# A transformer trunk layer on one core: the gate-and-up projections with the weight tiles stationary and the activations moving

## The chip, the cores and the metric

One core of a Trainium2 chip runs the whole layer in one launch. The metric is the device time of one execution in microseconds (us): the median of several runs of the same kernel. A profile is one execution, recorded instruction by instruction; its span runs from the first to the last instruction on the core.

## What is computed

The layer takes `x` (256 tokens of width 2048) and 256 memory tokens, all in float32. The change touches the two feed-forward blocks, one at the start and one at the end of the layer (`D_FF` is 5632):

```python
def rmsnorm(x, w):
    xf = x.astype(jnp.float32)
    y = xf * lax.rsqrt(jnp.mean(xf * xf, axis=-1, keepdims=True) + EPS)
    return (y * w.astype(jnp.float32)).astype(x.dtype)

def swiglu(x, w_gu, w_down):
    g, u = jnp.split(x @ w_gu, 2, axis=-1)
    return (jax.nn.silu(g) * u) @ w_down

h = h + 0.5 * rmsnorm(swiglu(rmsnorm(h, n_ffn1_pre), w_ffn1_gu, w_ffn1_down), n_ffn1_post)
# ... mixer: gated linear attention, gated delta rule, cross-attention, output projection ...
h = h + 0.5 * rmsnorm(swiglu(rmsnorm(h, n_ffn2_pre), w_ffn2_gu, w_ffn2_down), n_ffn2_post)
```

`w_gu` is 2048 x 11264: the gate half and the up half side by side. `w_down` is 5632 x 2048.

## The kernel before

**Units.** Every large product runs over units. A unit is a weight block of 256 rows by 512 columns (`UK` = 2 row tiles of 128, `CW` = 512), 512 KB in float32. There are 864 units in a fixed order; the table `PHASES` lists them by stage: `gu1` (176 units), `down1` (88), `mem` (32), `proj` (128), `gates0` (48), `up0` (24), `gates1` (48), `up1` (24), `out` (32), `gu2` (176), `down2` (88). SP issues the load of a unit into one of four ring slots (`raw`), ScalarE copies it to `whi` in the type fp32r (the high part, L869), VectorE writes `wlo` = `raw` - `whi` (L1275), and TensorE multiplies. A product is the sum of three: high by high, high by low, low by high. So a unit costs TensorE three products of the same size. The ring is four deep and the splits run four units ahead (`LOOK`): the slot of unit n is split again, for unit n + 4, as soon as TensorE has counted `unit_used` past n.

**A unit on TensorE** is the function `unit` (L469). The activations are stationary, one tile of 128 rows by 128 tokens, and the weights move, 512 columns at a time:

```python
for k in range(UK):
    for t in range(NT):
        cols = slice(t * P, (t + 1) * P)
        for m, (x, w) in enumerate(((hi, whi), (hi, wlo), (lo, whi))):
            ins = nc.tensor.matmul(acc[:, par, t, :], x[:, k0 + k, cols], w[:, s, k, :], ...)
```

That is 2 x 2 x 3 = 12 matmuls of 512 columns, and the result stands with tokens on the partitions. Each matmul is recorded as a weight load (LDWEIGHTS) and a MATMUL. Only the first matmul of a unit waits, for `lo_ready` and, at the start of a chunk, for its accumulator.

**The gate-and-up stages** (`gu` on each engine) run 11 iterations (`N_GU`) of 16 units each: eight units give the gate product for 512 hidden columns in accumulator 0, eight give the up product in accumulator 1. The first iteration is written out, the other ten are a hardware loop. ScalarE takes the gate product with Silu and the factor of the norm, a number for each token and thus for each partition (`rs`, L945). VectorE multiplies the up product by the same factor and by the gate (L1355), into `nat`. The activations of the next stage must have the hidden columns on the partitions, so TensorE transposes the 256 x 512 result in eight 128 x 128 tiles (`transposed`, L492 to L500). This is done two units later, after unit 2 of the next iteration (for the last iteration after unit 2 of `down`). Then ScalarE copies it to `act_hi` (L902) and VectorE forms `act_lo` (L1300).

**What sets the order.** Each engine runs its own written-out program and waits on counting semaphores. On ScalarE and VectorE the function `slots` goes through the units; the extra tasks of slot j stand behind ScalarE's split and ahead of VectorE's. The norm's factors come from GpSimd (`rsqrt`, L375 to L381), after ScalarE's squares and a sum on VectorE, in units 3 to 6 of the first iteration. In the first group of `proj`, a small product at L585 runs 48 matmuls of 256 columns in fp32r; the mixer's steps (L620 to L785) put small fp32 matmuls between units.

Of the kernel before, what the change touches and what calls it, by code (L numbers as in the profile page):

```python
# [70 lines left out]
T_X, T_ACT1, T_MEM, T_U, T_M, T_H2, T_ACT2 = 0, 4, 15, 19, 23, 27, 31  # L71
# [3 lines left out]
SPLIT_SMALL = 20  # L75
LOG_SCALE = -0.5 * math.log(GDN_D)


def hybrid_layer(nc, a, out, h_dram, mk_dram, mv_dram):
# [8 lines left out]
    with ExitStack() as ctx:  # L88
# [26 lines left out]


# [87 lines left out]
        junk = sb("junk", [P, CW], mybir.dt.bfloat16)  # L204

        acc = ctx.enter_context(nc.psum_tensor("acc", [P, 2, NT, CW], fp32))
        mix = ctx.enter_context(nc.psum_tensor("mix", [P, 4, CW], fp32))

# [259 lines left out]
        def _(pe):  # L468
# [66 lines left out]
            def down(f):  # L535
                base, q = UB[f"down{f + 1}"], QB[f"down{f + 1}"] // 2

                def between(j):
                    if j == 2 and i == 0:
                        pe.wait_ge(acc_out[1], q)  # L540
                        transposed((T_ACT1, T_ACT2)[f] + N_GU - 1, nat[:, :, CW:2 * CW], 0)
# [4 lines left out]
                    if i == 0 and j == U_F - 3:  # L546

                        pe.wait_ge(t_lo, half_tiles((T_ACT1, T_ACT2)[f] + N_GU))
# [30 lines left out]
            def small_steps(j):  # L579

                if j == 0:
                    pe.wait_ge(sem("wsm_lo"), 1)
# [4 lines left out]
                    ins.then_inc(sem("small_done"), 1)  # L587
                if j == 1:
                    pe.wait_ge(sem("small_T_ready"), 1)
                    for t in range(NT):  # L590
                        ins = nc.tensor.transpose(mix[:, 1, t * 32:(t + 1) * 32], small_T[:, t * P:(t + 1) * P], ident[0:32, 0:32])
                    ins.then_inc(sem("small_rows"), 1)
                if j == 3:
                    pe.wait_ge(sem("small_out"), 1)
                    for t in range(NT):
                        ins = nc.tensor.transpose(mix[0:RANK, 1, t * P:(t + 1) * P], small[:, t, 0:RANK], ident)
                    ins.then_inc(sem("lrT_done"), 1)
                if j == 7:

                    pe.wait_ge(sem("logdecay"), 1)  # L600
                    av = st[:, 0].rearrange("p t h -> p (t h)")
                    nc.tensor.matmul(mix[:, 2, 0:16], tri[:, :], av, start=True, stop=True)
                    nc.tensor.matmul(mix[:, 2, 16:32], ones[:, :], av, start=True, stop=True).then_inc(sem("gsum_done"), 1)
# [254 lines left out]
        def _(ac):  # L858
# [57 lines left out]
            def gu(f, i, first):  # L916
                n0, q = UB[f"gu{f + 1}"], QB[f"gu{f + 1}"] // 2

                def tasks(j):
# [11 lines left out]
                    if j == 2 and not first:  # L931
                        upper((T_ACT1, T_ACT2)[f] - 1 + i, act_hi[:, ds(i * 4 - 4, 4), :], 0)
                    if j == U_D - 1:
                        if first:
                            ac.wait_ge(sem("norm_rs"), (R_X, R_H2)[f] + 1)

                            ac.wait_ge(t_lo, half_tiles((T_X, T_H2)[f] + 4))
                            if f == 1:
                                ac.wait_ge(sem("h_stored"), 8 * 16)
                        ac.wait_ge(unit_used, at(n0, i, 2 * U_D, j) + 1)  # L940
                        if not first:

                            ac.wait_ge(acc_out[1], q + i)
# [4 lines left out]
                slots(n0, i, 2 * U_D, tasks)  # L948

# [4 lines left out]
            def down(f):  # L954
                n0, q = UB[f"down{f + 1}"], QB[f"down{f + 1}"] // 2

                def tasks(j):
                    if j == 2 and i == 0:
                        upper((T_ACT1, T_ACT2)[f] + N_GU - 1, act_hi[:, KT_F - 4:KT_F, :], 0)
# [18 lines left out]
            def memory():  # L978
                def tasks(j):
# [8 lines left out]
                    if j == SPLIT_SMALL:  # L988
# [3 lines left out]
                        act(wsmh[:, :, :], wsm[:, :, :], ACT.Copy).then_inc(sem("wsm_hi"), 1)  # L992
# [24 lines left out]
            def small_steps(j):  # L1017
                if j == 0:
                    ac.wait_ge(sem("small_done"), 1)
                    act(small_T[:, :], mix[0:32, 0, 0:SEQ], ACT.Copy).then_inc(sem("small_T_ready"), 1)  # L1020
                if j == 2:

                    ac.wait_ge(sem("norm_rs"), R_H1 + 1)
                    ac.wait_ge(sem("small_rows"), 1)
                    for t in range(NT):
                        ins = act(small[:, t, :], mix[:, 1, t * 32:(t + 1) * 32], ACT.Copy, scale=rs[:, R_H1, t:t + 1])
                    ins.then_inc(sem("small_out"), 1)
                    ac.wait_ge(sem("small_out"), 1)

                    act(stw[:, 0], small[:, :, RANK:RANK + GDN_H], ACT.Tanh, scale=0.5).then_inc(sem("tanh_b"), 1)  # L1030
                if j == 3:
                    ac.wait_ge(sem("lrT_done"), 1)
                    act(lrT[:, :], mix[0:RANK, 1, 0:SEQ], ACT.Copy).then_inc(sem("lrT_ready"), 1)

                    ac.wait_ge(sem("a_bias"), 1)
# [3 lines left out]
                    act(stw[:, 2], stw[:, 2], ACT.Ln, bias=1.0).then_inc(sem("softplus"), 1)  # L1039
                if j == 8:  # L1040
                    ac.wait_ge(sem("gsum_done"), 1)
                    act(stw[:, 3].rearrange("p t h -> p (t h)"), mix[:, 2, 0:16], ACT.Exp).then_inc(sem("exp_g"), 1)
                    ac.wait_ge(sem("g_rest"), 1)
                    act(st[:, 4], stw[:, 0], ACT.Exp).then_inc(sem("exp_rest"), 1)
# [223 lines left out]
        def _(ve):  # L1268
# [64 lines left out]
            def gu(f, i, first):  # L1333
# [3 lines left out]
                def tasks(j):  # L1337
# [6 lines left out]
                    if j == 2 and not first:  # L1344
                        rows = ds(i * 4 - 4, 4)
                        lower((T_ACT1, T_ACT2)[f] - 1 + i, act_lo[:, rows, :], act_hi[:, rows, :], 0)
                    if j == 2 * U_D - 1:
                        if first:
                            ve.wait_ge(sem("norm_rs"), k + 1)
                        ve.wait_ge(unit_used, at(n0, i, 2 * U_D, j) + 1)  # L1350

                        ve.wait_ge(acc_out[0], q + i + 1)
                        ve.wait_ge(t_done, (T_ACT1, T_ACT2)[f] + i)
# [4 lines left out]
                slots(n0, i, 2 * U_D, tasks)  # L1358

# [17 lines left out]
            def down(f):  # L1377
                n0, q = UB[f"down{f + 1}"], QB[f"down{f + 1}"] // 2

                def tasks(j):  # L1380
                    if j == 2 and i == 0:
                        lower((T_ACT1, T_ACT2)[f] + N_GU - 1, act_lo[:, KT_F - 4:KT_F, :], act_hi[:, KT_F - 4:KT_F, :], 0)
# [14 lines left out]
            def memory():  # L1397
                def tasks(j):
# [10 lines left out]
                    if j == SPLIT_SMALL:  # L1409
                        ve.wait_ge(sem("wsm_hi"), 1)  # L1410
                        tt(wsml[:, :, :], wsm[:, :, :], wsmh[:, :, :].bitcast(fp32), ALU.subtract).then_inc(sem("wsm_lo"), 1)
                slots(UB["mem"], 0, 4 * U_D, tasks)

            def small_steps(j):
                if j == 2:

                    ve.wait_ge(sem("tanh_b"), 1)
                    ts(st[:, 2], stw[:, 0], 0.5, 0.5, ALU.mult, ALU.add).then_inc(sem("beta"), 1)
                    tt(stw[:, 1], small[:, :, RANK + GDN_H:32], dtb[:, :].unsqueeze(1).broadcast_to([P, NT, GDN_H]),
                       ALU.add).then_inc(sem("a_bias"), 1)  # L1420
                if j == 4:

                    ve.wait_ge(sem("softplus"), 1)
                    stt(stw[:, 2], stw[:, 1], 0.0, stw[:, 2], ALU.max, ALU.add).then_inc(sem("softplus_sum"), 1)
                    ve.wait_ge(sem("softplus_sum"), 1)
                    stt(st[:, 0], stw[:, 2], -1.0, alog[:, :].unsqueeze(1).broadcast_to([P, NT, GDN_H]), ALU.mult,
                        ALU.mult).then_inc(sem("logdecay"), 1)
                if j == 8:

                    ve.wait_ge(sem("exp_g"), 1)  # L1430
                    nc.vector.tensor_copy(st[:, 1].rearrange("p t h -> p (t h)"), mix[:, 2, 0:16]).then_inc(sem("g_out"), 1)
                    ve.wait_ge(sem("g_out"), 1)
                    ve.wait_ge(sem("beta"), 1)
                    tt(stw[:, 0], mix[:, 2, 16:32].rearrange("p (t h) -> p t h", t=NT), st[:, 1], ALU.subtract).then_inc(sem("g_rest"), 1)
                    stt(st[:, 3], st[:, 2], -1.0, stw[:, 3], ALU.mult, ALU.mult).then_inc(sem("neg_beta"), 1)
                    ve.wait_ge(sem("neg_beta"), 1)
                    ve.wait_ge(sem("exp_rest"), 1)
# [279 lines left out]
```

## Time and profile before

| | |
|---|---|
| median of 3 runs | 2577.98 us (2576.51 to 2579.25) |
| span of the profiled execution | 2574.7 us |
| TensorE matmul, busy | 2549.0 us, 99% |
| TensorE weight load, busy | 2122.4 us, 82% |
| VectorE busy | 1367.1 us, 53% |
| ScalarE busy | 1237.7 us, 48% |
| weight traffic, mean | 186 GB/s |

No time other than its span is given for the profiled execution; the median of the runs lies 3.3 us above the span. In the profile's rows a matmul's own duration includes its time in the pipeline, so that matmuls overlap and their durations add up to more than the engine's busy time. What a matmul costs in a stream is the distance from its start to the next one's start. PE is the row of matmuls, PEld that of weight loads.

### The profile page before, as it was taken

To read this page: it belongs to the slowest core of one execution; us is meant where nothing else is said; L and a number is where in the kernel's file an instruction comes from. 1 tells how busy PE (TensorE), PEld (TensorE's weight loads), DVE (VectorE), ACT (ScalarE), POOL (GpSimd) and SP (SyncE) were. 2 spreads that over 40 slices of the span, in tenths; PEclk is the share of its full clock that TensorE was granted. 3 is DMA by queue.
4 is the path that set the end of the run, shared out by engine and by line. 5 is a ranking of instruction groups with operands and counts; after the bars stand their busy time and mean duration, and the time that the engine had idled before them with its cause. 6 is when DMAs were issued, how large, how long until landed. Compare 5 with 4: busy or idle time off the path is not lost.

```text
span 2574.7 us, 33533 instructions
## 1 busy us (share of the span) xinstructions
PE 2549.0 (99%) x11883; PEld 2122.4 (82%) x11883; DVE 1367.1 (53%) x1473; ACT 1237.7 (48%) x1490; POOL 79.9 (3%) x119
## 2 busy tenths in 40 slices
PE   8999999999999999999999999999999999999998
PEld 7888888888888888888888888888788888888886
DVE  5444454554455456666665564465554444544444
ACT  5444444454445564747475544444544444444442
POOL 3000000000011000101010000000100000000000
PEclk9999999999999999999999999999999999999999
DMA  7666666656677654545454666665666666666654
GB/s 248 189 188 187 190 185 194 188 197 194 193 236 247 189 164 131 155 130 152 125 149 130 188 188 194 193 239 191 189 194 188 189 187 189 187 193 238 195 191 146
DMA packets 286022, 478.90 MB, mean 186 GB/s; under 512 B 17389, under 2 KB 91249, under 8 KB 285169
## 3 DMA queue, kind: packets, MB, share of 16 engines
q1 hardware_dynamic: 279648, 455.16, 58.8%
q0 software_dynamic: 5200, 20.50, 2.3%
q10 hardware_dynamic: 1088, 2.10, 0.3%
q8 instruction: 55, 0.90, 0.1%
q14 instruction: 31, 0.25, 0.0%
HBM read 469.30 MB, written 8.39 MB: 186 GB/s over the span
## 4 chain that ended last, share of the span: by engine, by line
PE 98%; ACT 1%; DVE 1%; DMA 0%; issue 0%; POOL 0%; POOLq 0%; DVEq 0%; ACTq 0%
PE acc L481 91%; PE mix L500 1%; PE mix L709 1%; PE mix L698 1%; PE mix L732 1%; PE mix L702 0%; PE mix L651 0%; DVE nat L1330 0%; PE mix L684 0%; PE mix L585 0%; PE mix L620 0%; DMA nat<-x 0%; ACT whi L869 0%; PE mix L665 0%; PE mix L664 0%
## 5 line engine op out<-in xcount | busy, mean ns | idle before, releaser
L1275 DVE TENSOR_TENSOR wlo<-raw,whi 128x1024 fp32r<-128x1024 f32 x860 | 1050.9, 1224 | 894.5 <-ACT whi L869 891.0
L869 ACT ACTIVATE whi<-raw 128x1024 fp32r<-128x1024 f32 x860 | 910.6, 1060 | 1240.8 <-PE acc L481 1213.7
L481 PE MATMUL acc<-whi,x_hi 128*128 128x512 f32 x1664 | 651.0, 391 | 0.3 <-DVE wlo L1662 0.3
L481 PE MATMUL acc<-whi,x_lo 128*128 128x512 f32 x1664 | 648.1, 389 | 0.0
L481 PE MATMUL acc<-wlo,x_hi 128*128 128x512 f32 x1664 | 647.6, 389 | 0.0
L481 PEld LDWEIGHTS acc<-whi,x_lo 128*128 128x128 f32 x1664 | 312.5, 188 | 65.3
L481 PEld LDWEIGHTS acc<-whi,x_hi 128*128 128x128 f32 x1664 | 312.8, 188 | 64.3 <-issue 0.7
L481 PEld LDWEIGHTS acc<-wlo,x_hi 128*128 128x128 f32 x1664 | 312.7, 188 | 63.9
L481 PE MATMUL acc<-whi,u_hi 128*128 128x512 f32 x896 | 361.7, 404 | 0.0
L481 PE MATMUL acc<-whi,u_lo 128*128 128x512 f32 x896 | 349.9, 390 | 0.0
L481 PE MATMUL acc<-wlo,u_hi 128*128 128x512 f32 x896 | 349.2, 390 | 0.0
L481 PE MATMUL acc<-whi,act_hi 128*128 128x512 f32 x704 | 274.4, 390 | 0.0
L481 PE MATMUL acc<-whi,act_lo 128*128 128x512 f32 x704 | 273.9, 389 | 0.0
L481 PE MATMUL acc<-wlo,act_hi 128*128 128x512 f32 x704 | 273.9, 389 | 0.0
L481 PEld LDWEIGHTS acc<-whi,u_lo 128*128 128x128 f32 x896 | 168.2, 188 | 36.2
L481 PEld LDWEIGHTS acc<-whi,u_hi 128*128 128x128 f32 x896 | 168.5, 188 | 34.2 <-issue 2.3
L481 PEld LDWEIGHTS acc<-wlo,u_hi 128*128 128x128 f32 x896 | 168.6, 188 | 33.3 <-issue 1.0
L481 PEld LDWEIGHTS acc<-whi,act_lo 128*128 128x128 f32 x704 | 132.1, 188 | 27.6
L481 PEld LDWEIGHTS acc<-whi,act_hi 128*128 128x128 f32 x704 | 132.2, 188 | 27.5
L481 PEld LDWEIGHTS acc<-wlo,act_hi 128*128 128x128 f32 x704 | 132.2, 188 | 27.0
L481 PE MATMUL acc<-whi,o_hi 128*128 128x512 f32 x192 | 74.9, 390 | 0.0
L481 PE MATMUL acc<-whi,o_lo 128*128 128x512 f32 x192 | 74.7, 389 | 0.0
(300 smaller groups left out, 1422.9 us busy)
## 6 DMA issues: line engine op xcount, KB each, us to landing
raw<-w_ffn_gu SPq DMA_DIRECT2D x352, 512.0 KB
raw<-w_ffn_down SPq DMA_DIRECT2D x176, 512.0 KB
raw<-w_in SPq DMA_DIRECT2D x224, 256.0 KB
raw<-w_in SPq DMA_DIRECT2D x96, 512.0 KB
raw<-w_mem_kv SPq DMA_DIRECT2D x32, 512.0 KB
raw<-w_out SPq DMA_DIRECT2D x32, 512.0 KB
raw<-w_in SPq DMA_DIRECT2D x64, 128.0 KB
raw<-w_up_gla SPq DMA_DIRECT2D x16, 512.0 KB
```

Source lines behind the costliest of these rows:

```text
L481: ins = nc.tensor.matmul(acc[:, par, t, :], x[:, k0 + k, cols], w[:, s, k, :], start=first and k == 0 and m == 0, stop=last and k == UK - ...
L500: ins = nc.tensor.transpose(v[:, blk, t * P:(t + 1) * P], src[:, t, blk * P:(blk + 1) * P], ident)
L698: ins = nc.tensor.matmul(m4(0)[:, u, :], lmat[:, u, :], xinv[:, u, :], start=True, stop=True)
L709: ins = nc.tensor.matmul(m4(1)[:, u, :], tinv[:, u, :], zb[:, u, :], start=True, stop=True)
L732: ins = nc.tensor.matmul(m4(3)[:, 2 * li + t, :], k_, q_, start=True, stop=True)
L869: act(whi[:, s], raw[:, s], ACT.Copy).then_inc(hi_ready, 1)
L1275: tt(wlo[:, s], raw[:, s], whi[:, s].bitcast(fp32), ALU.subtract).then_inc(lo_ready, 1)
```

## The change

The gate-and-up stages use a new function `unit_t`. The other stages keep `unit`. In `unit_t` the weight tile of 128 x 128 is stationary and the activations move, 256 columns (all tokens) at a time. The product comes out with the hidden columns on the partitions and the tokens along the free dimension, which is the layout that the down stage reads.

- Per unit: 2 x 4 x 3 = 24 matmuls of 256 columns in place of 12 of 512.
- The eight transposes of an iteration go, 22 times in all (11 for each feed-forward block). `act_hi` and `act_lo` are formed straight from the product.
- The norm's factor now differs along the free dimension. Two transposes of a broadcast `rs` column (`spread_norm`, once for each block, after unit 9) and a ScalarE copy give it as a 128 x 256 tile `rsb`.
- The take-out is split otherwise: VectorE multiplies the gate product by `rsb` out of PSUM (slot 7, in the first iteration slot 10), ScalarE applies Silu in SBUF, VectorE multiplies by `rsb` again (one slot later), and in slot 15 by the up product. `act_hi` and `act_lo` are made in slot 1 of the next iteration.
- 20 semaphores that each served once are merged into three (`once`). This moves no instruction.

```diff
@@ TensorE
+            def unit_t(n, j, k0, par, first, last, before):
+                s = j % RING
+                pe.wait_ge(lo_ready, n + 1)
+                if first and (not isinstance(before, int) or before > 0):
+                    pe.wait_ge(acc_out[par], before)
+                for k in range(UK):
+                    for c in range(4):
+                        cols = slice(c * P, (c + 1) * P)
+                        for m, (x, w) in enumerate(((x_hi, whi), (x_lo, whi), (x_hi, wlo))):
+                            ins = nc.tensor.matmul(accT[:, par, c, :], w[:, s, k, cols], x[:, k0 + k, :],
+                                                   start=first and k == 0 and m == 0 and c % 2 == 0,
+                                                   stop=last and k == UK - 1 and m == 2, skip_group_check=True)
+                ins.then_inc(unit_used, 1)
+            def spread_norm(k):
+                pe.wait_ge(sem("norm_rs"), k + 1)
+                pe.wait_ge(t_lo, half_tiles((T_X if k == R_X else T_H2) + 4))
+                if k == R_X:
+                    pe.wait_ge(sem("vecT_ready"), 3)
+                for t in range(NT):
+                    ins = nc.tensor.transpose(mix[:, 3, t * P:(t + 1) * P], rs[:, k, t:t + 1].broadcast_to([P, P]), ident)
+                ins.then_inc(sem("rsb_rows"), 1)
@@ gu
-                    if j == 2 and not first:
-                        pe.wait_ge(acc_out[1], q + i)
-                        transposed((T_ACT1, T_ACT2)[f] - 1 + i, nat[:, :, CW:2 * CW], 0)
...
+                    if first and j == U_D + 1:
+                        spread_norm((R_X, R_H2)[f])
-                for half in range(2):
-                    chunk(at(base, i, 2 * U_D, half * U_D), half * U_D, U_D, x_hi, x_lo, half, q + i, between)
+                for j in range(2 * U_D):
+                    unit_t(at(base, i, 2 * U_D, j), j, UK * (j % U_D), j // U_D, j % U_D == 0, j % U_D == U_D - 1, q + i)
+                    between(j)
@@ down
-                    if j == 2 and i == 0:
-                        pe.wait_ge(acc_out[1], q)
-                        transposed((T_ACT1, T_ACT2)[f] + N_GU - 1, nat[:, :, CW:2 * CW], 0)
...
+                pe.wait_ge(sem("act_lo_ready"), (f + 1) * N_GU - 1)
@@ ScalarE, gu
-                    if j == 2 and not first:
-                        upper((T_ACT1, T_ACT2)[f] - 1 + i, act_hi[:, ds(i * 4 - 4, 4), :], 0)
-                    if j == U_D - 1:
...
-                        for t in range(NT):
-                            ins = act(nat[:, t, 0:CW], acc[:, 0, t, :], ACT.Silu, scale=rs[:, (R_X, R_H2)[f], t:t + 1])
-                        ins.then_inc(acc_out[0], 1)
+                    if j == 1 and not first:
+                        upper_act(f, i - 1)
+                    if first and j == U_D + 1:
+                        ac.wait_ge(sem("rsb_rows"), f + 1)
+                        act(rsb[:, :], mix[:, 3, 0:SEQ], ACT.Copy).then_inc(sem("rsb_ready"), 1)
+                    if j == (U_D + 2 if first else U_D - 1):
+                        ac.wait_ge(acc_out[0], q + i + 1)
+                        act(gated, gated, ACT.Silu).then_inc(sem("gate_silu"), 1)
@@ VectorE, gu
-                    if j == 2 and not first:
-                        rows = ds(i * 4 - 4, 4)
-                        lower((T_ACT1, T_ACT2)[f] - 1 + i, act_lo[:, rows, :], act_hi[:, rows, :], 0)
+                    if j == 1 and not first:
+                        lower_act(f, i - 1)
+                    if j == (U_D + 2 if first else U_D - 1):
...
+                        ve.wait_ge(unit_used, at(n0, i, 2 * U_D, U_D - 1) + 1)
+                        tt(gated, accT[:, 0], rsb4, ALU.mult).then_inc(acc_out[0], 1)
+                    if j == (U_D + 3 if first else U_D):
+                        ve.wait_ge(sem("gate_silu"), done + 1)
+                        tt(gated, gated, rsb4, ALU.mult).then_inc(sem("gate_done"), 1)
                     if j == 2 * U_D - 1:
...
-                        for t in range(NT):
-                            ins = stt(nat[:, t, CW:2 * CW], acc[:, 1, t, :], rs[:, k, t:t + 1], nat[:, t, 0:CW], ALU.mult, ALU.mult)
-                        ins.then_inc(acc_out[1], 1)
+                        ve.wait_ge(sem("gate_done"), done + 1)
+                        tt(prod, accT[:, 1], gated, ALU.mult).then_inc(acc_out[1], 1)
```

TensorE's instructions at the end of unit 2 and the start of unit 3 in the hardware loop of the first feed-forward block, before (L481 is `unit`, L500 `transposed`; a matmul's name is output <- the two inputs, its size the moving operand's):

```order
242 L481 MATMUL acc<-wlo,x_hi 128x512
243 L481 MATMUL acc<-whi,x_lo 128x512
244 L496 ISA [waits acc_out1]
245 L500 MATMUL mix<-masks,nat 128x128 [waits t_lo]
246 L500 MATMUL mix<-masks,nat 128x128 x7
247 L473 REGISTER_ALU
248 L481 MATMUL acc<-whi,x_hi 128x512 [waits lo_ready]
249 L481 MATMUL acc<-wlo,x_hi 128x512
```

The boundary between two units of that loop in the changed kernel, which is now the same behind every unit of the loop (L512 is `unit_t`):

```order
447 L512 MATMUL acc<-x_lo,whi 128x256
448 L512 MATMUL acc<-x_hi,wlo 128x256
449 L505 REGISTER_ALU
450 L512 MATMUL acc<-x_hi,whi 128x256 [waits lo_ready]
451 L512 MATMUL acc<-x_lo,whi 128x256
```

The transposes and their wait are gone; nothing else stands between units.

VectorE in the same loop, slots 7 and 8, in the changed kernel (L1311 is the split into `wlo`, L1391 and L1394 are the two products with `rsb`; before, only splits stood here):

```order
45 L1311 TENSOR_TENSOR wlo<-raw,whi 128x1024 [waits hi_ready]
46 L1391 TENSOR_TENSOR nat<-acc,rsb 128x1024 [waits unit_used]
47 L1310 REGISTER_ALU
48 L1311 TENSOR_TENSOR wlo<-raw,whi 128x1024 [waits hi_ready]
49 L1393 REGISTER_ALU
50 L1394 TENSOR_TENSOR nat<-nat,rsb 128x1024 [waits gate_silu]
51 L1310 REGISTER_ALU
52 L1311 TENSOR_TENSOR wlo<-raw,whi 128x1024 [waits hi_ready]
```

The two products now stand ahead of the splits of slots 7 and 8, and the second waits for ScalarE's Silu.

## Rows read from the trace of the kernel before

**Rows 1.** The page: granted TensorE clock in 40 slices, in tenths of full speed.
```profile
PEclk9999999999999999999999999999999999999999
```
**Rows 2.** The page: the chain that ended last, its share by engine.
```profile
PE 98%; ACT 1%; DVE 1%; DMA 0%; issue 0%; POOL 0%; POOLq 0%; DVEq 0%; ACTq 0%
```
**Rows 3.** Timeline, ScalarE's splits: start us, us, engine line op, out<-in, count [idle before].
```profile
94.97 1.06 ACT L869 ACTIVATE whi<-raw 128x1024 fp32r<-128x1024 f32 x1 [1.66 <-PE acc L481]
...
108.57 1.06 ACT L869 ACTIVATE whi<-raw 128x1024 fp32r<-128x1024 f32 x1 [1.66 <-PE acc L481]
```
**Rows 4.** Timeline of PE around the transposes of two gate-and-up iterations.
```profile
66.43 0.39 PE L481 MATMUL acc<-whi,x_lo 128*128 128x512 f32 x1
66.66 1.03 PE L500 MATMUL mix<-masks,nat 128*128 128x128 f32 x8
67.45 0.48 PE L481 MATMUL acc<-whi,x_hi 128*128 128x512 f32 x1
67.77 0.39 PE L481 MATMUL acc<-wlo,x_hi 128*128 128x512 f32 x1
...
111.10 1.03 PE L500 MATMUL mix<-masks,nat 128*128 128x128 f32 x8
```
**Rows 5.** Timeline of PE around the 48 matmuls of L585.
```profile
841.82 0.39 PE L481 MATMUL acc<-whi,u_lo 128*128 128x512 f32 x1
842.05 0.28 PE L585 MATMUL mix<-u_hi,wsmh 128*32 128x256 f32 x1
...
847.39 0.28 PE L585 MATMUL mix<-u_lo,wsmh 128*32 128x256 f32 x1
847.50 0.40 PE L481 MATMUL acc<-whi,u_hi 128*128 128x512 f32 x1
```
**Rows 6.** Timeline of the weight loads (PEld) at the two ends of L585's run.
```profile
841.83 0.11 PEld L585 LDWEIGHTS mix<-u_hi,wsmh 128*32 128x32 f32 x1
...
847.39 0.19 PEld L481 LDWEIGHTS acc<-whi,u_hi 128*128 128x128 f32 x1
```
**Rows 7.** Timeline of PE in the mixer: fp32 matmuls of 128 columns, each with its load.
```profile
1002.95 1.05 PE L698 MATMUL mix<-sq,yr 128*128 128x128 f32 x8
1003.84 0.60 PE L702 MATMUL mix<-masks,sq 128*128 128x128 f32 x4
1004.28 1.06 PE L732 MATMUL mix<-gq,ge 128*128 128x128 f32 x8
```
**Rows 8.** Timeline of PE around a pair of small transposes (L520, L521).
```profile
39.24 0.22 PE L520 MATMUL mix<-masks,vec 68*128 68x68 f32 x1
...
39.64 0.39 PE L481 MATMUL acc<-wlo,x_hi 128*128 128x512 f32 x1
```
**Rows 9.** Groups by line and form, VectorE: busy us, mean ns | idle before.
```profile
L1275 DVE TENSOR_TENSOR wlo<-raw,whi 128x1024 fp32r<-128x1024 f32 x860 | 1050.9, 1224 | 894.5 <-ACT whi L869 891.0 <-DVE st L1435 0.3
L1355 DVE SCALAR_TENSOR_TENSOR nat<-acc,rs,nat 128x512 f32<-128x512 f32 x44 | 31.0, 746 | 13.3 <-PE acc L481 13.3
L1300 DVE TENSOR_TENSOR act_lo<-mix,act_hi 128x1024 f32 x20 | 24.5, 1224 | 52.0 <-ACT act_hi L902 52.0
```
**Rows 10.** Groups by line and form, ScalarE.
```profile
L869 ACT ACTIVATE whi<-raw 128x1024 fp32r<-128x1024 f32 x860 | 910.6, 1060 | 1240.8 <-PE acc L481 1213.7 <-DMA raw<-w_in 8.5 <-DMA raw<-w_mem_kv 7.3
```
**Rows 11.** Timeline: GpSimd's norm factor and PE's last matmul of unit 9, both blocks.
```profile
37.94 1.74 POOL L381 TENSOR_TENSOR rs<-rsw,halfn 128x2 f32<-128x2 f32 x1
...
41.95 0.39 PE L481 MATMUL acc<-whi,x_lo 128*128 128x512 f32 x1
...
1857.96 1.73 POOL L381 TENSOR_TENSOR rs<-rsw,halfn 128x2 f32<-128x2 f32 x1
...
1861.75 0.39 PE L481 MATMUL acc<-whi,x_lo 128*128 128x512 f32 x1
```
**Rows 12.** Register and semaphore instructions of TensorE's sequencer at L473: ns min/median/max.
```profile
L473 PEldq ALU_OP  x393: 32/32/42, 57.2 to 2315.8; - x197
L473 PEldq EVENT_SEMAPHORE  x21: 51/51/51, 12.0 to 2373.8; - x21
```

More of the change, by code:

```diff
@@ L114, in sem, with once @@
             return sems[name]
+        def once(name):
+            for of, names in ONCE.items():
+                if name in names:
+                    return sem(of), names.index(name) + 1
         raw = sb("raw", [P, RING, UK, CW])
@@ L581, in small_steps @@
                 if j == 0:
-                    pe.wait_ge(sem("wsm_lo"), 1)
+                    pe.wait_ge(*once("wsm_lo"))
                     for k in range(KT_D):
@@ L586, in small_steps @@
                                                    start=k == 0 and m == 0, stop=k == KT_D - 1 and m == 2)
-                    ins.then_inc(sem("small_done"), 1)
+                    ins.then_inc(once("small_done")[0], 1)
                 if j == 1:
-                    pe.wait_ge(sem("small_T_ready"), 1)
+                    pe.wait_ge(*once("small_T_ready"))
                     for t in range(NT):
                         ins = nc.tensor.transpose(mix[:, 1, t * 32:(t + 1) * 32], small_T[:, t * P:(t + 1) * P], ident[0:32, 0:32])
-                    ins.then_inc(sem("small_rows"), 1)
+                    ins.then_inc(once("small_rows")[0], 1)
                 if j == 3:
-                    pe.wait_ge(sem("small_out"), 1)
+                    pe.wait_ge(*once("small_out"))
                     for t in range(NT):
                         ins = nc.tensor.transpose(mix[0:RANK, 1, t * P:(t + 1) * P], small[:, t, 0:RANK], ident)
-                    ins.then_inc(sem("lrT_done"), 1)
+                    ins.then_inc(once("lrT_done")[0], 1)
                 if j == 7:
-                    pe.wait_ge(sem("logdecay"), 1)
+                    pe.wait_ge(*once("logdecay"))
                     av = st[:, 0].rearrange("p t h -> p (t h)")
                     nc.tensor.matmul(mix[:, 2, 0:16], tri[:, :], av, start=True, stop=True)
-                    nc.tensor.matmul(mix[:, 2, 16:32], ones[:, :], av, start=True, stop=True).then_inc(sem("gsum_done"), 1)
+                    nc.tensor.matmul(mix[:, 2, 16:32], ones[:, :], av, start=True, stop=True).then_inc(once("gsum_done")[0], 1)
             def mixer_steps(slot, g):
@@ L930, in tasks, with upper_act @@
                         ac.wait_ge(sem("vecT_ready"), 3)
[L931 to L946 removed]
+                    if j == 1 and not first:
[6 more added lines that the diff above has]
+                        act(gated, gated, ACT.Silu).then_inc(sem("gate_silu"), 1)
                 slots(n0, i, 2 * U_D, tasks)
+            def upper_act(f, i):
+                ac.wait_ge(acc_out[1], QB[f"gu{f + 1}"] // 2 + i + 1)
+                act(act_hi[:, ds(i * 4, 4), :], prod, ACT.Copy).then_inc(sem("act_hi_ready"), 1)
             def first_upper(f, c):
@@ L957, in tasks @@
                 def tasks(j):
-                    if j == 2 and i == 0:
-                        upper((T_ACT1, T_ACT2)[f] + N_GU - 1, act_hi[:, KT_F - 4:KT_F, :], 0)
+                    if j == 1 and i == 0:
+                        upper_act(f, N_GU - 1)
                     if f == 0 and i == 0 and j in (3, 8, 13, 18):
@@ L991, in tasks @@
                         ac.wait_ge(sem("wsm_in"), 2 * 16)
-                        act(wsmh[:, :, :], wsm[:, :, :], ACT.Copy).then_inc(sem("wsm_hi"), 1)
+                        act(wsmh[:, :, :], wsm[:, :, :], ACT.Copy).then_inc(once("wsm_hi")[0], 1)
                     if j % U_D == U_D - 1:
@@ L1038, in small_steps @@
                     st_step(act(alog[:, :], alog[:, :], ACT.Exp))
-                    act(stw[:, 2], stw[:, 2], ACT.Ln, bias=1.0).then_inc(sem("softplus"), 1)
+                    act(stw[:, 2], stw[:, 2], ACT.Ln, bias=1.0).then_inc(once("softplus")[0], 1)
                 if j == 8:
[L1041 to L1044, printed above, removed]
+                    ac.wait_ge(*once("gsum_done"))
+                    act(stw[:, 3].rearrange("p t h -> p (t h)"), mix[:, 2, 0:16], ACT.Exp).then_inc(once("exp_g")[0], 1)
+                    ac.wait_ge(*once("g_rest"))
+                    act(st[:, 4], stw[:, 0], ACT.Exp).then_inc(once("exp_rest")[0], 1)
             def mixer_steps(slot, g):
@@ L1380, in tasks @@
                 def tasks(j):
-                    if j == 2 and i == 0:
-                        lower((T_ACT1, T_ACT2)[f] + N_GU - 1, act_lo[:, KT_F - 4:KT_F, :], act_hi[:, KT_F - 4:KT_F, :], 0)
+                    if j == 1 and i == 0:
+                        lower_act(f, N_GU - 1)
                     if f == 0 and i == 0 and j == 3:
@@ L1409, in tasks @@
                     if j == SPLIT_SMALL:
-                        ve.wait_ge(sem("wsm_hi"), 1)
-                        tt(wsml[:, :, :], wsm[:, :, :], wsmh[:, :, :].bitcast(fp32), ALU.subtract).then_inc(sem("wsm_lo"), 1)
+                        ve.wait_ge(*once("wsm_hi"))
+                        tt(wsml[:, :, :], wsm[:, :, :], wsmh[:, :, :].bitcast(fp32), ALU.subtract).then_inc(once("wsm_lo")[0], 1)
                 slots(UB["mem"], 0, 4 * U_D, tasks)
@@ L1415, in small_steps @@
                 if j == 2:
-                    ve.wait_ge(sem("tanh_b"), 1)
-                    ts(st[:, 2], stw[:, 0], 0.5, 0.5, ALU.mult, ALU.add).then_inc(sem("beta"), 1)
+                    ve.wait_ge(*once("tanh_b"))
+                    ts(st[:, 2], stw[:, 0], 0.5, 0.5, ALU.mult, ALU.add).then_inc(once("beta")[0], 1)
                     tt(stw[:, 1], small[:, :, RANK + GDN_H:32], dtb[:, :].unsqueeze(1).broadcast_to([P, NT, GDN_H]),
-                       ALU.add).then_inc(sem("a_bias"), 1)
+                       ALU.add).then_inc(once("a_bias")[0], 1)
@@ L1436, in small_steps @@
-                    ve.wait_ge(sem("neg_beta"), 1)
-                    ve.wait_ge(sem("exp_rest"), 1)
+                    ve.wait_ge(*once("exp_g"))
+                    nc.vector.tensor_copy(st[:, 1].rearrange("p t h -> p (t h)"), mix[:, 2, 0:16]).then_inc(once("g_out")[0], 1)
+                    ve.wait_ge(*once("g_out"))
+                    ve.wait_ge(*once("beta"))
+                    tt(stw[:, 0], mix[:, 2, 16:32].rearrange("p (t h) -> p t h", t=NT), st[:, 1], ALU.subtract).then_inc(once("g_rest")[0], 1)
@@ L1439, in mixer_steps @@
+                    stt(st[:, 3], st[:, 2], -1.0, stw[:, 3], ALU.mult, ALU.mult).then_inc(once("neg_beta")[0], 1)
+                    ve.wait_ge(*once("neg_beta"))
+                    ve.wait_ge(*once("exp_rest"))
             def mixer_steps(slot, g):
```

59 lines of the change are left out of this document (34 added, 25 removed).

## The prediction

> **What bounds the kernel now.** I first read the table of busy times: TensorE is busy for 99% of the span, the other engines for about half. The chain that ended last says the same: 98% of it is TensorE's [rows 2]. The granted clock stays in its top tenth throughout, the 2.4 GHz level [rows 1]. So the time is TensorE's own work, and anything on another engine counts only if TensorE comes to wait for it.
>
> Next I want the price of a unit. ScalarE starts a split each time TensorE has finished a unit, and sat idle for 1.66 us before each one. From 94.97 to 108.57 us are five units: 2.72 us each [rows 3]. That is 12 matmuls at 226.7 ns. 512 columns at 2.4 GHz would be 213.3 ns, so the stream costs 17/16 of a cycle per column here. The weight loads are recorded with 0.19 us each [rows 6] and lie wholly beside the stream, since nothing is added to the 226.7.
>
> A gate-and-up iteration is 16 units, 16 x 2.72 = 43.52 us. From one group of transposes to the next the timeline has 111.10 - 66.66 = 44.44 us [rows 4]. The missing 0.9 us is the transposes. No other hole is left in the loop: waits and the loop's branch cost nothing now.
>
> **Part 1: the transposes go.** After the matmul at 66.43 the next unit's first would start at 66.66 and its second at 66.88. With the eight transposes between, they start at 67.45 and 67.77 [rows 4]. That is 0.79 us for the transposes and 0.09 us for the first matmul behind them, which takes 0.32 until the next instead of 0.23. The iteration's own difference is 0.9 us, and I take that: 22 x 0.9 = 19.8 us off TensorE's path. All of it counts, since TensorE waits for nothing there.
>
> **Part 2: two small transposes for each block come.** Rows exist for such a pair: L520 starts at 39.24, where the next unit would have begun, and that unit's second matmul starts at 39.64 instead of 39.47 [rows 8]. With a few slower matmuls behind it I take 0.23 us, so 0.5 us for the two blocks. They wait for GpSimd's factor, which is there at 39.7 us in block 1 and at 1859.7 in block 2, while the last matmul of unit 9 starts at 41.95 and 1861.75 [rows 11]. Both are covered by 2 us. If that cover were gone, the price would be the lateness itself, twice.
>
> **Part 3: 4224 matmuls of 512 columns become 8448 of 256.** 352 units x 12 and x 24. The total of columns is the same. The question is only the distance from start to start of a 256-column matmul in fp32r whose stationary tile has 128 columns. No row has exactly this in a stream, so I bound it:
>
> - L585 streams 256 columns in fp32r, but with 32 stationary columns. From 842.05 to 847.50 are 48 matmuls: 113.5 ns each, with two at 0.12 at the start [rows 5]. Half of 226.7 is 113.3.
> - Does the surcharge of a sixteenth come from the weight load? Then it would change with the load. The last 512-column matmul before L585 has a load of 32 columns beside it (0.11 us) and still takes 842.05 - 841.82 = 0.23. The last 256-column matmul of L585 has a full load of 128 columns beside it (0.19 us, started with it at 847.39), and still takes 847.50 - 847.39 = 0.11 [rows 5, 6]. So the surcharge goes with the columns streamed, and a full load can be hidden by 256 columns, at least once.
> - Can loads of 128 columns follow each other that fast? In the mixer, 12 fp32 matmuls of 128 columns, each with its own load of 128, go from 1002.95 to 1004.28: 111 ns each, across a boundary with a wait [rows 7]. This bounds the load's own pace at 111 ns, if fp32r loads are paced like fp32 ones, and it is 2 ns below what the stream takes.
>
> I take 113.3 ns, since the only fp32r row of 256 columns has it and both bounds on the load lie at or below it. Part 3 then costs nothing. The low end of this term is the mixer's 111 ns: 8448 x 2.3 = 19 us less. The high end is the 118 ns of L585's first two matmuls (0.12 in the rows): 8448 x 4.7 = 40 us more.
>
> Here a rule speaks against the change. The Trainium skill ("TensorE: Matmul & The Clock Gate", section "The mechanism" of its part on packing small matmuls) says that weight loads overlap running matmuls only when the row groups differ. All tiles here use all rows, so every added load would be exposed; it is rival D below. The trace contradicts it, by that 226.7 ns with a full load inside.
>
> **Part 4: ScalarE and VectorE.** A VectorE pass over 1024 columns takes 1.22 us [rows 9]. Beside the 16 splits, an iteration had two passes of 0.75 and one of 1.22, 2.7 us; it now has four of about 1.22, 4.9 us. ScalarE has two passes over 1024 columns, near 1.06 us each [rows 10], in place of one and two halves, so it stays as it was. In slots 7 and 8, with T the end of unit 7: VectorE's first product ends at T + 1.3. ScalarE has split by T + 1.06 [rows 10] and finishes Silu near T + 2.4. Meanwhile VectorE splits, until T + 2.5, and does its second product until T + 3.7. The next split's input is there at T + 2.72 + 1.06 = T + 3.8. So nothing is late, and even a late split has slack: the slot refilled after unit n is read three units later, 8.2 us. SP's loads wait for VectorE's split and could start a microsecond later in two slots; the ring holds four units. I cost this part at nothing. What covers it is TensorE's 2.72 us for each unit.
>
> The merged semaphores order the same instructions and cost nothing. The new wait ahead of `down` is for a step finished in slot 1, 14 units earlier.
>
> **Sum.** 2574.7 - 19.8 + 0.5 = 2555.4 us of span. The median lies 3.3 above the span, so 2558.7 us, 0.75% less than 2577.98.
>
> **Rivals.**
>
> - **B, the load just misses its shadow.** A few ns for each of 8448 matmuls decide everything. The saving of 19.3 us is gone at 19.3/8448 = 2.3 ns, thus at 115.6 ns. Between about 115.0 and 116.2 ns the result is no change (0.2% of the time, 5.2 us, is about what a measurement of this kernel can tell). For it: the margin between the stream and the load's pace in rows 7 is only 2 ns, those rows are fp32, and no row has the two together twice running. At 118 ns the time would be 2558.7 + 40 = 2598 us: **slower**.
> - **C, TensorE's sequencer shows between units.** Each unit has a register instruction and a wait, of 32 and 51 ns [rows 12]. Now they hide beside matmuls of 227 ns; the shadow becomes half as long. If both were exposed for each unit: 352 x 83 ns = 29 us, so 2588 us, slower. It decides from 55 ns per unit. Against it: in rows 7 three groups, with waits between, run at 111 ns.
> - **D, loads serial.** A load of 0.19 us that begins when the previous matmul starts and must end before the next would set 188 ns: 8448 x 75 = 630 us more, about 3190 us. The 111 ns of rows 7 and the 0.11 us at 847.39 speak against it.
> - **E, the shorter stream is cheaper per column** and runs at the 111 ns of rows 7: 2558.7 - 19 = 2540 us. L585 at exactly half speaks against it.
> - **F, a new wait.** TensorE waits for the factor or for a late split. For one wait per iteration to take the whole gain it would have to be 0.9 us long, and rows 11 and Part 4 leave 2 us and more.
>
> **How the numbers follow.** The forecast (113.3 to under 115.0 ns, no new stall): 0.77. B gives 0.06 for no change and 0.07 for slower. C: 0.04 slower. D: 0.02. E: 0.02, faster. F: 0.02, no change. So faster by over 0.2% 0.79, the same 0.08, slower 0.13. The predicted time is the forecast's, 2559 us. For the range: the forecast's own is 2557 to 2573 us (up to 1.67 ns more per matmul). I take in a little of E below and the cases of no change above, and stop at 2578; what is left out is B and C where they are slower, D, and most of E, 0.15 or so.
>
> **What would show it.** In the profile after: matmuls of `unit_t` 0.11 us apart and units 2.72 us apart; an iteration of 43.5 us; no L500-like group in the loop; weight loads busy for nearly all of the gate-and-up stretches, yet not setting the pace; VectorE some 50 us busier; ScalarE's wait for TensorE still the longest. Rival B would show as a steady distance over 115 ns inside a unit, C as one longer distance at each unit's start. I am wrong about the size of Part 1 if an iteration had more or less than 0.9 us of transposes, and wrong in kind if the distance of 256-column matmuls with full loads is not half of 226.7.

## The result: 1.4% slower

| | before | changed |
|---|---|---|
| median of 4 runs | 2578.51 us (2576.51 to 2579.25) | 2613.75 us (2613.61 to 2615.11) |
| span of the profiled execution | 2574.7 us | 2611.9 us |

The ratio is 1.0141, with a 95% interval of 1.0126 to 1.0155. The profiled execution of the changed kernel took 2613.61 us itself, 1.7 us more than its span. The prediction was 2559 us, with a range that ended at 2578 us. The time went the other way.

The page of the changed kernel: busy times, granted clock, and the chain that ended last.

```profile
PE 2586.6 (99%) x15935; PEld 2327.8 (89%) x15935; DVE 1412.9 (54%) x1495; ACT 1235.3 (47%) x1470; POOL 78.4 (3%) x119
...
PEclk9999999999999999999999999999999999999999
...
PE 98%; ACT 1%; DVE 0%; DMA 0%; issue 0%; POOL 0%; POOLq 0%; ACTq 0%; DVEq 0%
```

Nothing new bounds the kernel. TensorE is busy for 99% as before, in the same tenth of the clock [rows 1], and the chain is TensorE's for 98% [rows 2]. Only its work has grown. The next view shows where: TensorE's timeline inside a unit of the loop (start us, us, engine, line), matmuls first and then the weight loads of the same stretch.

```profile
299.87 0.28 PE L512 MATMUL acc<-x_hi,wlo 128*128 128x256 f32 x1
299.99 0.28 PE L512 MATMUL acc<-x_hi,whi 128*128 128x256 f32 x1
300.11 0.28 PE L512 MATMUL acc<-x_lo,whi 128*128 128x256 f32 x1
300.23 0.28 PE L512 MATMUL acc<-x_hi,wlo 128*128 128x256 f32 x1
300.35 0.28 PE L512 MATMUL acc<-x_hi,whi 128*128 128x256 f32 x1
300.47 0.28 PE L512 MATMUL acc<-x_lo,whi 128*128 128x256 f32 x1
```

```profile
299.87 0.19 PEld L512 LDWEIGHTS acc<-x_hi,whi 128*128 128x128 f32 x1
299.99 0.19 PEld L512 LDWEIGHTS acc<-x_lo,whi 128*128 128x128 f32 x1
```

Five distances from 299.87 to 300.47: **120 ns** each, where I had taken 113.3. It is steady: between 230 and 530 us all 2436 distances in the trace are 119 to 121 ns, at unit boundaries too. ScalarE's splits, which start when a unit ends, give the same per unit (the counterpart of [rows 3]):

```profile
93.55 1.06 ACT L908 ACTIVATE whi<-raw 128x1024 fp32r<-128x1024 f32 x1 [1.82 <-PE acc L512]
...
107.95 1.06 ACT L908 ACTIVATE whi<-raw 128x1024 fp32r<-128x1024 f32 x1 [1.82 <-PE acc L512]
```

Five units in 14.40 us are 2.88 us each, 0.16 more than before. 352 units x 0.16 = 56.3 us. Take off the 19.3 us that Parts 1 and 2 were to give, and 37.0 us remain. The two spans differ by 37.2 us and the medians by 35.2. Every run lies about 2 us above its own span, so the profiled execution of the kernel before, with a span of 2574.7 us, was among its shortest; the 1.8 us between 37.0 and 35.2 are within the spread of its runs. So the whole result is two numbers, and one of them was mis-sized.

The other parts went as costed. VectorE's groups by line (busy us, mean ns | idle before):

```profile
L1391 DVE TENSOR_TENSOR nat<-acc,rsb 128x1024 f32<-128x1024 f32 x22 | 26.9, 1224 | 11.3 <-PE acc L512 11.3
L1394 DVE TENSOR_TENSOR nat<-nat,rsb 128x1024 f32<-128x1024 f32 x22 | 27.0, 1226 | 2.3 <-ACT nat L977 2.3
L1398 DVE TENSOR_TENSOR nat<-acc,nat 128x1024 f32<-128x1024 f32 x22 | 26.9, 1224 | 12.3 <-PE acc L512 12.3
```

The new wait for Silu cost VectorE 2.3 us over 22 times, hidden beside TensorE. VectorE is 45.8 us busier (1412.9 against 1367.1); I had said some 50. The pair of transposes for the norm's factor, on TensorE's timeline in block 1 (compare [rows 8]):

```profile
44.07 0.28 PE L512 MATMUL acc<-x_hi,wlo 128*128 128x256 f32 x1
44.19 0.38 PE L524 MATMUL mix<-masks,rs 128*128 128x128 f32 x2
44.32 0.36 PE L512 MATMUL acc<-x_hi,whi 128*128 128x256 f32 x1
44.53 0.28 PE L512 MATMUL acc<-x_lo,whi 128*128 128x256 f32 x1
```

Without the pair the unit's second matmul would stand at 44.31; it stands at 44.53. That is 0.22 us, against 0.23 assumed, with no wait ahead.

### The profile page after: what moved, and what is told of

Read it like the earlier page. It is cut to its first block, busy times and chain, and to the rows that moved or that the text cites. A ratio compares the mean times of both kernels' runs of the same rounds, so it can differ in the third digit from the quotient of the medians.

```text
span 2611.9 us, 41594 instructions
## 1 busy us (share of the span) xinstructions
PE 2586.6 (99%) x15935; PEld 2327.8 (89%) x15935; DVE 1412.9 (54%) x1495; ACT 1235.3 (47%) x1470; POOL 78.4 (3%) x119
## 4 chain that ended last, share of the span: by engine, by line
PE 98%; ACT 1%; DVE 0%; DMA 0%; issue 0%; POOL 0%; POOLq 0%; ACTq 0%; DVEq 0%
PE acc L496 53%; PE acc L512 39%; PE mix L748 1%; PE mix L737 1%; PE mix L541 1%; PE mix L771 1%; PE mix L741 0%; DMA nat<-x 0%; PE mix L690 0%; DVE nat L1366 0%; PE mix L723 0%; PE mix L624 0%; PE mix L659 0%; ACT whi L908 0%; PE mix L704 0%
## 5 line engine op out<-in xcount | busy, mean ns | idle before, releaser
L1311 DVE TENSOR_TENSOR wlo<-raw,whi 128x1024 fp32r<-128x1024 f32 x860 | 1049.0, 1224 | 867.2 <-ACT whi L908 864.1
L512 PE MATMUL acc<-x_hi,whi 128*128 128x256 f32 x2816 | 799.7, 284 | 0.0
L512 PE MATMUL acc<-x_lo,whi 128*128 128x256 f32 x2816 | 798.7, 284 | 0.0
L512 PE MATMUL acc<-x_hi,wlo 128*128 128x256 f32 x2816 | 798.6, 284 | 0.0
L512 PEld LDWEIGHTS acc<-x_hi,whi 128*128 128x128 f32 x2816 | 542.3, 193 | 0.4 <-issue 0.4
L512 PEld LDWEIGHTS acc<-x_lo,whi 128*128 128x128 f32 x2816 | 542.2, 193 | 0.0
L512 PEld LDWEIGHTS acc<-x_hi,wlo 128*128 128x128 f32 x2816 | 542.1, 193 | 0.0
L496 PE MATMUL acc<-whi,x_hi 128*128 128x512 f32 x256 | 100.3, 392 | 0.0
L496 PE MATMUL acc<-whi,x_lo 128*128 128x512 f32 x256 | 99.8, 390 | 0.0
```

Of the source, the lines that this page charges most:

```text
L512: ins = nc.tensor.matmul(accT[:, par, c, :], w[:, s, k, cols], x[:, k0 + k, :], start=first and k == 0 and m == 0 and c % 2 == 0, stop=las ...
L1311: tt(wlo[:, s], raw[:, s], whi[:, s].bitcast(fp32), ALU.subtract).then_inc(lo_ready, 1)
```

## The experiments

After the result two theories of the 120 ns were open, and a third on the exchange of the operands' roles.

**1. Streams alone.** A kernel that runs nothing but streams of matmuls. Each stage is one loop:

```diff
+            # (128, 256, 'sta', 'mov')
+            for i in range(96):
+                o, w, x = args(4, 1 * i + 0, 128, 256, sta, mov)
+                ins = mm(o, w, x, start=i == 0 and 0 == 0, stop=i == 95 and 0 == 0, skip_group_check=True)
```

> A kernel of its own that leaves the whole layer out: only streams of 96 matmuls on TensorE (stationary columns M, moving columns N, in fp32r, fp32 and bf16), no other engine working beside them. Theory 1, pace of the loads: a stream of fp32r matmuls costs 17/16 of a cycle per moving column, and full loads of 128 columns cannot follow each other faster than 120 ns. Then with M = 128: N = 448, 384, 320 take 198.3, 170.0, 141.7 ns from start to start; N = 256, 192 and 128 all take 120; M = 96, 64 or 32 with N = 256 take 113.3; M = 32 with N = 512 takes 226.7; alternating M = 128 and 32 at N = 256 takes 113.3 each; alternating N = 512 and 256 at M = 128 takes 226.7 + 113.3 = 340 per pair. Theory 2, a surcharge for each matmul that depends on its own stationary columns: 13.3 ns at 128, 6.7 ns at 32, whatever N is. Then N = 448, 384, 320, 192 take 200.0, 173.3, 146.7, 93.3 ns (if the loads allow it), M = 32 with N = 512 takes 220, alternating M takes 116.7 on average, alternating N takes 346.7 per pair. fp32 at N = 128: 111 ns, as in the layer.

Groups by line and form (128*128 is rows and columns of the stationary tile, then the moving operand; busy us, mean ns; the trace shows fp32r as f32). The distance from start to start is (busy - mean) / (count - 1), to the rounding of the rows:

```profile
L62 PE MATMUL acc<-mov,sta 128*128 128x512 f32 x96 | 21.9, 389 | 0.0
...
L70 PE MATMUL acc<-mov,sta 128*128 128x384 f32 x96 | 16.8, 334 | 0.0
...
L74 PE MATMUL acc<-mov,sta 128*128 128x320 f32 x96 | 14.2, 309 | 0.0
...
L78 PE MATMUL acc<-mov,sta 128*128 128x256 f32 x96 | 11.7, 283 | 0.0
...
L98 PE MATMUL acc<-mov,sta 128*32 128x256 f32 x96 | 11.0, 276 | 0.0
...
L82 PE MATMUL acc<-mov,sta 128*128 128x192 f32 x96 | 10.9, 274 | 0.0
L86 PE MATMUL acc<-mov,sta 128*128 128x128 f32 x96 | 10.9, 274 | 0.0
L130 PE MATMUL acc<-stb 128*128 128x256 bf16 x96 | 10.6, 273 | 0.0
...
L110 PE MATMUL acc<-mov,sta 128*32 128x128 f32 x96 | 5.9, 223 | 0.0
L134 PE MATMUL acc<-stb 128*128 128x128 bf16 x96 | 5.5, 219 | 0.0
```

From the starts in the trace, in ns, with the first few of each stream left out, and beside them what is left over the columns' own time at 2.4 GHz:

| stationary columns, type | moving columns | start to start | over the columns |
|---|---|---|---|
| 128, fp32r | 512 | 226.7 | 13.3 |
| 128, fp32r | 448 | 202.7 | 16.0 |
| 128, fp32r | 384 | 173.3 | 13.3 |
| 128, fp32r | 320 | 146.7 | 13.3 |
| 128, fp32r | 256 | 120.0 | 13.3 |
| 128, fp32r | 192 and 128 | 111.7 and 111.6 | load's pace |
| 96, fp32r | 256 | 116.0 | 9.3 |
| 64 or 32, fp32r | 256 | 113.3 | 6.7 |
| 64, fp32r | 512 | 229.9 | 16.6 |
| 32, fp32r | 512 | 231.7 | 18.3 |
| 32, fp32r | 128 | 60.0 | 6.7 |
| 128, bf16 | 256 | 109.2 | 2.5 |
| 128, bf16 | 128 | 55.8 | 2.5 |

Theory 1 falls. Full loads of fp32r follow each other at 111.7 ns (192 and 128 moving columns), not 120. And the surcharge is not a sixteenth of the columns: at 384 and 320 it is the same 13.3 ns as at 512. Theory 2 holds in its main part: the surcharge is paid per matmul. Alternating 128 and 32 stationary columns gave the 116.7 on average that it asked for, alternating 512 and 256 moving columns gave 230.0 and 116.7, together 346.7 as it asked, and one of 512 followed by two of 256 gave 466.7 for the three, which is 226.7 + 2 x 120. Its second part is wrong: with 32 stationary columns the 6.7 ns hold at 256 and 128 moving columns, but at 512 the surcharge is 18.3 ns, the highest of all.

**2. The kernel before, with its matmuls cut in two.** The change's count of matmuls without its exchange of roles, and with all transposes kept.

```diff
+                        if halves:
+                            for v in range(2):
+                                part = slice(v * SEQ, (v + 1) * SEQ)
+                                for m, (x, w) in enumerate(((hi, whi), (hi, wlo), (lo, whi))):
+                                    ins = nc.tensor.matmul(acc[:, par, t, part], x[:, k0 + k, cols], w[:, s, k, part],
...
```

> The kernel before, with each matmul of the gate-and-up units cut into two of 256 moving columns; the activations stay stationary, the transposes stay. If the number of matmuls is the cause (theories 1 and 2 alike): 8448 x 6.7 ns = 57 us more than before, 2635 us. Theory 3, the exchange of the roles is the cause (freshly written weights as stationary operand, transposed product): no change, 2578 us, and the matmuls stand 113.3 ns apart.

Measured: 2633.19 us against 2578.46 for before on the same chip, ratio 1.0211 (1.0194 to 1.0229), 54.7 us more. Its timeline in the loop:

```profile
299.83 0.28 PE L484 MATMUL acc<-wlo,x_hi 128*128 128x256 f32 x1
299.95 0.28 PE L484 MATMUL acc<-whi,x_lo 128*128 128x256 f32 x1
...
300.43 0.28 PE L484 MATMUL acc<-whi,x_hi 128*128 128x256 f32 x1
300.55 0.28 PE L484 MATMUL acc<-wlo,x_hi 128*128 128x256 f32 x1
```

120 ns again (0.72 us for six). Theory 3 falls: which operand is stationary does not matter, the number of matmuls does. This also gives the rest of the change by itself: the changed kernel differs from this one in the transposes, the roles and the take-out, but not in the size or number of its matmuls. 2613.75 - 2633.19 = -19.4 us. I had costed these parts at -19.8 + 0.5 = -19.3.

**3. The kernel before, with one transpose of each eight.**

```diff
-                for blk in range(4):
-                    for t in range(NT):
+                for blk in range(1 if few else 4):
+                    for t in range(1 if few else NT):
                         ins = nc.tensor.transpose(v[:, blk, t * P:(t + 1) * P], src[:, t, blk * P:(blk + 1) * P], ident)
```

> The kernel before, but of each group of eight transposes of the gate-and-up product only one is done (seven of eight tiles of the activations are left out, so the layer's values are not computed). If the groups stand on TensorE's path as I costed them: 22 x 7 x 0.109 us = 16.8 us less, 2562 us. Rival: part of the groups was hidden or what follows them costs as much: under 8 us less, 2571 us or more.

Measured: 2563.30 us against 2578.46, ratio 0.9942 (0.9925 to 0.9958). That is 15.2 us less (10.8 to 19.3 by the interval), near the 16.8 and beyond the rival's 8. The traces are sharper: from one group of the loop to the next it is 44.43 us before and 43.67 here, 0.76 us for seven transposes of 0.109. The groups of transposes did stand on TensorE's path.

**4. What the surcharge hangs on.** Streams alone again, with one thing varied at a time.

```diff
+            # a same stationary
+            for i in range(96):
+                c, o = (i * 128) % (2 * D), (i * 256) % (2 * D - 512)
+                ins = mm(acc[:, 3, 0:256], sta[0:128, 0:0 + 128], mov[0:128, o:o + 256], start=i < 2, stop=i > 93, skip_group_check=True)
```

> Streams alone again, the layer left out, all fp32r at 256 moving columns unless said. Known by now: 120 ns at 128 stationary columns, 113.3 at 32, 106.7 for the columns themselves. If the surcharge belongs to the matmul's own stationary tile (theory 2): in the pattern 128, 32, 32, 32 one distance in four is 120 and three are 113.3, mean 115.0; in 32, 128, 128, 128 the mean is 118.3; alternating 128 and 32 at 512 moving columns the mean is between 220 and 230. If it belongs to the load running beside, the long distance is one place earlier, with the same means. If it belongs to a change of the stationary tile's contents, the stream with the same tile each time takes less than 120; if to writing one PSUM bank, the stream over two banks takes less; if to the rows or the moving data's address, 64 rows or the same moving data do. I expect 120 in all four. 480 moving columns: 213.3 (200 + 13.3); 288, 272: 133.3, 126.7; 240, 224, 208: 113.3 or the load's 111.7, whichever is longer. 480 matmuls in a row of the form of the changed kernel: 120 to the end.

```profile
L151 PE MATMUL acc<-mov,sta 128*128 128x256 f32 x480 | 57.8, 283 | 0.0
...
L97 PE MATMUL acc<-mov,sta 64*128 64x256 f32 x96 | 11.8, 281 | 0.0
L89 PE MATMUL acc<-mov,sta 128*128 128x256 f32 x96 | 11.7, 283 | 0.0
L93 PE MATMUL acc<-mov,sta 128*128 128x256 f32 x96 | 11.7, 283 | 0.0
```

The same stationary tile every time (L89), two PSUM banks in turn (L93) and 64 rows (L97) all took 120.0 ns; the same moving data took 120.0 too (in three of these streams the first distance alone is longer, 200 to 223 ns: L97, L151 and the one with the same moving data). 480 matmuls in a row (L151) stayed at 120. So none of these carries the surcharge. The question of own tile or load beside stays open: the pattern 128, 32, 32, 32 took 116.7 on average, not 115.0, and its distances are 113 to 120 in an order that fits neither answer; 32, 128, 128, 128 took 118.3 as both answers ask. 128 and 32 in turn at 512 columns took 230.0 on average, the upper end of what was said. A mixed stream spreads the surcharge instead of showing whose it is. The sizes between missed by a few ns as well: 480 columns took 216.7 (I said 213.3), 288 and 272 took 131.7 and 125.3 (133.3 and 126.7), 240 took 112.0. With 112, 80 and 48 stationary columns at 256 it was 117.8, 113.3 and 113.3. The surcharge of full tiles from 256 columns up lies between 12 and 17 ns and is not in proportion to the columns: 11.7 at 288, 13.3 at 384, 16.7 at 480, 13.3 at 512. With narrow tiles it does grow with them: 64 stationary columns took 173.3 ns at 384 moving columns, 13.3 over, between their 6.7 at 256 and 16.6 at 512.

**5 and 6. The same two kernels in bf16.** In the first study bf16 had only 2.5 ns over its columns. If that is so in the layer, the change must gain there. Both kernels get the same edit.

```diff
-    f32r = mybir.dt.float32r
+    f32r = mybir.dt.bfloat16
...
```

The lines not shown keep the size of the shared memory areas and take out the casts that read fp32r as fp32.

> The kernel before with all high and low parts in bf16 in place of fp32r (the same three products, with fewer bits). In the first study bf16 took 216 ns at 512 columns and 109.2 at 256, with 2.5 ns over the columns' own time. So 10368 matmuls x (226.7 - 216) = 111 us less: about 2467 us. Theory that the 13.3 ns hang on the width of 128 stationary columns in any type: no change.

> The changed kernel with the same exchange of the type. If only fp32r has the surcharge of 13.3 ns per matmul: against e5_before_bf16, 8448 x 109.2 - 4224 x 216 = 10 us more for the matmuls and 19.3 us less for the transposes, so 9 us less than e5_before_bf16, about 2458 us: the change turns into a gain. If the surcharge or the pace of the loads is the same in bf16: 37 us more than e5_before_bf16.

The old layout in bf16 took 2462.40 us (4 runs, 2461.64 to 2466.55), ratio to before 0.9557 (0.9541 to 0.9573): 115 us less, where 111 were expected; no run traces the other 4. The new layout in bf16 took 2453.98 us (4 runs, 2453.01 to 2455.28), ratio 0.9521 (0.9505 to 0.9537). The pair differs by 8.4 us, where 9 were expected, and their runs do not overlap. Here are their timelines in the loop, first the new layout, then the old:

```profile
299.81 0.27 PE L516 MATMUL acc<-x_hi,whi 128*128 128x256 bf16 x1
299.92 0.27 PE L516 MATMUL acc<-x_lo,whi 128*128 128x256 bf16 x1
...
300.35 0.27 PE L516 MATMUL acc<-x_hi,wlo 128*128 128x256 bf16 x1
300.46 0.27 PE L516 MATMUL acc<-x_hi,whi 128*128 128x256 bf16 x1
```

```profile
299.72 0.38 PE L485 MATMUL acc<-whi,x_lo 128*128 128x512 bf16 x1
299.94 0.38 PE L485 MATMUL acc<-whi,x_hi 128*128 128x512 bf16 x1
...
300.58 0.38 PE L485 MATMUL acc<-whi,x_hi 128*128 128x512 bf16 x1
```

109 ns for 256 columns (0.65 us for six), 215 for 512 (0.86 for four). The same change that loses 35 us in fp32r gains 8 in bf16. Both bf16 kernels are faster than the fp32r ones at the price of fewer bits, so they are a test of the cause and not a replacement.

## Why the prediction was wrong, step by step

**What bounds the kernel: right.** TensorE alone, before and after. "The granted clock stays in its top tenth throughout" read the row of slices too finely: a slice is 64 us long, and at the start of the second block the granted clock is 0.50 for 6.8 us in both kernels (from 1826.1 us before, from 1845.3 us after). Both pay it, so the difference is untouched.

**Part 1, the transposes: right.** Costed at 19.8 us. Run 2 puts Parts 1 and 2 together at 19.4 us, and run 3 shows seven of eight transposes at 0.76 us in each iteration.

**Part 2, the pair for the norm's factor: right**, 0.22 us against 0.23 in block 1, and no wait.

**Part 3, the distance between matmuls: this is the step that failed.** The sentence was "the surcharge goes with the columns streamed". I had two sizes, 226.7 ns at 512 columns and 113.3 at 256, and read them as one slope. But the row at 256 had a stationary tile of 32 columns, where the surcharge is 6.7 ns, half of 13.3 for another reason. A fixed cost per matmul and a cost per column fit those two rows alike; with full tiles at 256, 320, 384 and 512 columns, run 1 shows the fixed one, 13.3 ns each time. The two readings at the ends of L585's run were of the load beside a matmul. They never varied the matmul's length with its own tile held: the 512-column matmul there had a stationary tile of 128 columns, the 256-column one of 32 [rows 5, 6]. The term was put at 0, and it measured 8448 x 6.67 = 56.3 us (120.0 ns against 113.3). My upper end of 118 ns lay below it too.

**Part 4, ScalarE and VectorE: right**, all hidden.

**The rivals.** B came nearest. It had the place and the sign, "a few ns for each of 8448 matmuls decide everything", and the right threshold: 120 is beyond its 115.6 ns. Its mechanism, a load that misses its shadow, is not what happens at 256 columns, since the loads can follow at 111.7 ns. I gave it 0.07 for slower, too little for a term where no row had the shape in question and 2.3 ns were the whole gain. C did not happen: the distance at a unit's start is 120 like the others. D did not happen either: loads of 0.19 us are begun every 0.12 us. On the rule of the Trainium skill ("TensorE: Matmul & The Clock Gate", section "The mechanism"), that loads overlap running matmuls only when the row groups differ, the trace disagrees as before: the loads run beside matmuls that stand 120 ns apart.

**The range: wrong.** It left out B's slow side. The 3.3 us between span and median, which the sum used, were not a cost of every run either, as said above, but that is 1.5 us at most. With ends that far apart around a threshold of 2.3 ns, the term's uncertainty was larger than the gain that I forecast.

## What to carry to other kernels

Before you cut a long stream of matmuls into twice as many short ones, price one matmul in exactly the new shape (both operands' sizes and the type) and multiply by the count; two rows that differ in more than one size do not give a slope. In fp32r, 512 moving columns with a full stationary tile cost 226.7 ns and two of 256 cost 240, so an exchange of operands that halves the moving side must save more than 13 ns per old matmul elsewhere. In bf16 the same cut cost about 2.6 ns per old matmul ((19.3 - 8.4) us over 4224), and dropping the transposes was worth it.

## What the runs showed that I had not expected

- An fp32r matmul with a full tile costs 12 to 17 ns over its columns at 2.4 GHz from 256 columns up, whatever their number; bf16 at 256 and 128 costs 2.5. In the layer this is shown at 512 and 256 columns only, the other sizes in the streams alone. What inside TensorE causes it stays open. The same tile, other banks, half the rows and the same moving data were tried and change nothing.
- It is gone at the low clock. The changed kernel's first microseconds:

```profile
11.99 0.41 PE L512 MATMUL acc<-x_lo,whi 128*128 128x256 f32 x1
...
15.62 0.34 PE L512 MATMUL acc<-x_hi,whi 128*128 128x256 f32 x1
```

  17 distances in 3.63 us are 213.5 ns each, and 256 columns at 1.2 GHz are 213.3. The level is inferred here from the distances: the profile gives a granted clock of 1.00 for 12 to 15.6 us, but the trace has no record of the clock before 15.7 us, where the distances fall to 120. One pair of such matmuls lies in a stretch that is recorded as low (busy time of each engine, then the granted clock, 0.50, the DMA share and GB/s); TensorE had stood idle for 5.3 us up to 1847.36:

```profile
1845.30:1852.10 6.80, 4.25 (x19) 3.85 (x20) 5.72 (x10) 1.84 (x5) 2.11 (x3) 0.50 0.46 137
```

```profile
1851.80 0.42 PE L512 MATMUL acc<-x_lo,whi 128*128 128x256 f32 x1
1852.01 0.32 PE L512 MATMUL acc<-x_hi,wlo 128*128 128x256 f32 x1
```

  They stand 213 ns apart too.
- A stationary tile of 32 columns is cheaper by 6.7 ns at 256 moving columns (113.3 against 120.0) but dearer by 5.0 ns at 512 (231.7 against 226.7).
- In plain fp32 one matmul stands as two records. Run 1 issued 96 fp32 matmuls of 256 columns:

```profile
L118 PE MATMUL acc<-xin 128*128 128x256 f32 x192 | 41.6, 379 | 0.0
```

  192 records, 215.8 ns from one to the next: 432 ns for one matmul, four cycles per column at 2.4 GHz, 3.6 times fp32r's 120. So what the prediction called 12 matmuls in [rows 7] were four matmuls in eight records and four transposes. Their 12 loads at 111 ns each are the same reading, and run 1 found 111.7 for fp32r and for fp32.
- Loads of 128 columns in fp32r are recorded with 188 to 192 ns, yet follow each other at 111.7 ns; the recorded duration does not give the pace.
